# Gathered expert rows: a row is added one panel after its product, and its buffer is filled again one panel after that

## The chip, the cores and the metric

The kernel runs on 1 core of one Trainium2 chip. The metric is the device time of one execution in microseconds (us), the median over runs; lower is better. The engines are called PE (TensorE, matrix products), DVE (VectorE), ACT (ScalarE), POOL (GpSimd) and SP (SyncE, which only issues DMAs here).

## The reference

Two transformer-like blocks run on 512 tokens of width 1024, batch 1, all in float32. The change touches one part of the first block, the product-key experts (PEER). Each token makes 8 queries; each query picks 16 of 16384 experts and has a softmax gate for each pick. An expert is one row of `expert_u` and one row of `expert_v`:

```
u = expert_u[idx]                                   # idx: 128 tokens x 8 heads x 16 picks
v = expert_v[idx]
act = gelu(einsum("thkd,td->thk", u, xt))
out = einsum("thk,thkd->td", gate * act, v)
```

So for each token and each of its 128 picks: the dot product of a row of `expert_u` with the token, a gelu, a product with the gate, and a row of `expert_v` scaled by that number and summed. What comes before (a hybrid of a linear recurrence and convolutions) and after (feed-forward layers, an mLSTM, dilated attention, attention to a memory) is not touched.

## The kernel before

**Two ways to the same sum.** For 384 of the 512 tokens the kernel computes all 16384 experts as dense matrix products and multiplies with a gate table that is zero where nothing was picked. For the other 128 tokens (one on each partition) it gathers the picked rows from memory: 128 picks per token, `PICKS = 128`. The gathered work runs beside the dense work, on engines that the dense work leaves some time.

**The dense work** goes in weight panels of 128 partitions x 1024 floats (512 KB). SP loads panel p into one of 4 places of `weight_ring` (`load_panel`) as soon as POOL is through with panel p-4. ACT copies the panel in two halves to `weight_high`, rounded to fp32r (L249, L251: the split's high part; it may overwrite a place once PE has used panel p-2). POOL subtracts this from the panel and so makes `weight_low`, again in two halves (L277, one pair a panel). PE multiplies the high part with the high and low parts of the input (L291, L292, 16 matmuls) and the low part with the high part of the input (L298, 8 matmuls). A panel is one step.

The gathered work is spread over the steps of three stages, in one count of steps:
- steps 0 to 15, late panels: products with `expert_u`, whose gelu ACT makes and SP stores away (parked);
- steps 16 to 111, parked panels, 12 groups of 8: products with `expert_v`. In each step DVE makes one chunk of the next group's input, by three gate operations (L1592 multiplies a parked activation with its gate, L1596 rounds it to fp32r, L1598 takes the rest; not in the last group), then does its gathered work (`use_rows`), then adds a finished bank to the residual (L1681), for which it waits until PE is through with that panel;
- from step 112, 4 groups of 16: 8 panels of `expert_u`, after each of which ACT makes a gelu and DVE the gates (L1856, L1860, L1862), and 8 of `expert_v`, after each of which DVE adds to the residual (L1873). PE needs all eight gates of a group at its middle.

**The gathered work** of pick k has four parts. Three tables of step numbers, made at L1480 to L1494, say when each stands in its engine's instructions:
- the fetch (`fetch_rows`, L1529), an indirect DMA that POOL issues: for each of 128 tokens a row of 2048 floats (u and v), 1 MB, into buffer k % 4 of `picked_rows`. It stands at step `FETCH_AT[k]`, behind POOL's pair of splits of that step. It waits until the buffer's last user, pick k-4, is added;
- the dot (`use_rows`, L1540), DVE, at step `DOT_AT[k]`;
- gelu and gate (`weigh_rows`, L1555, L1558), ACT, at step `DOT_AT[k] + 1`, behind ACT's split for the next panel. ACT waits for the dot;
- the add (`use_rows`, L1546), DVE, at step `ADD_AT[k]`: the row of v, scaled, is added to a sum in PSUM. It waits for ACT's weight. In a step that has both, the add of the earlier pick stands ahead of the dot.

The step numbers of the dots are spread evenly, with a weight of 0.8 on the parked steps, so that there about three steps in four have a dot.

All engines run through their own instructions in order. They are tied by semaphores only; nothing sets the order but these tables and loops.

Of the kernel before, what the change touches and what calls it, by code (L numbers as in the profile page):

```python
# [1089 lines left out]
PICKS = HEADS * TOPK // COPIES  # L1090
# [5 lines left out]
ROWS = 4  # L1096
# [380 lines left out]
LAST_GROUP_STEP = FIRST_EXPERT_STEP + (EXPERT_GROUPS_LEFT - 1) * 2 * EXPERT_GROUP  # L1477

FIRST_DOT = 5
LAST_DOT = LAST_GROUP_STEP - 2  # L1480
PARKED_SHARE = 0.8


def dot_steps():

    weights = [PARKED_SHARE if LATE_STEPS <= step < FIRST_EXPERT_STEP else 1.0 for step in range(FIRST_DOT, LAST_DOT + 1)]
    reached = np.cumsum(weights) / sum(weights) * (PICKS - 1)
    return [FIRST_DOT + int(np.searchsorted(reached, k + 1e-9)) for k in range(PICKS - 1)] + [LAST_DOT]


DOT_AT = dot_steps()
ADD_AT = [at + 2 for at in DOT_AT]
FETCH_AT = [0] * ROWS + [min(ADD_AT[k - ROWS] + 2, DOT_AT[k]) for k in range(ROWS, PICKS)]
assert all(FETCH_AT[k] <= DOT_AT[k] for k in range(PICKS)) and ADD_AT[-1] == LAST_GROUP_STEP  # L1494


# [26 lines left out]
def fetch_rows(m, pool, io, picked, step):  # L1523

    for k in range(PICKS):
        if FETCH_AT[k] == step:
            if k >= ROWS:
# [6 lines left out]
def use_rows(m, dve, picked, step):  # L1534

    for k in range(PICKS):
        halves = picked.rows[:, k % ROWS, :].rearrange("p (w a n) -> p w a n", w=2, a=2)
        if DOT_AT[k] == step:
# [3 lines left out]
                .then_inc(picked.dotted, 1)  # L1542
        if ADD_AT[k] == step:
            dve.wait_ge(picked.weighed, k + 1)
# [1854 lines left out]
```

## Time and profile before

| | |
|---|---|
| median of 3 runs | 3851.97 us (3847.91 to 3859.61) |
| profiled execution, own time | 3855.03 us |
| its span | 3853.2 us |
| PE busy | 3639.1 us (94%) |
| DVE busy | 2125.1 us (55%) |
| ACT busy | 1509.6 us (39%) |
| POOL busy | 1920.2 us (50%) |
| first and last fetch L1529, start | 856.9 and 1575.3 us |
| first and last add L1546, start | 891.9 and 1591.5 us |

The shares are means over the whole span, in which stages with different limits follow one another; the gathered work lies in less than a fifth of it. Times in the trace are counted from the span's start. The late panels start at about 854 us, the parked panels at 928 us, the last four groups at about 1362 us. Ends of matmuls are modelled, and a POOL operation's span is rough.

### The profile page before, as it was taken

The page shows a single profiled execution, that of the slowest core. Times are in us where ns is not written, and L with a number is a line of the kernel's source. Part 1 is how long each engine was busy: PE and PEld are TensorE (multiplying, and loading weights), DVE is VectorE, ACT ScalarE, POOL GpSimd, SP SyncE. Part 2 cuts the span into 40 slices and gives each one's busy share as a digit, 9 for nine tenths or more (in the row PEclk, how much of TensorE's full clock was granted, in tenths as well). Part 3 has the DMA queues.
Part 4 walks back from the last instruction along what each step waited for, and adds up shares of the span by engine and source line. Part 5 has one row for each costly group of instructions (what it writes and reads, how often), then busy time and mean ns, then how long its engine had stood idle before and what let it go on. Part 6 is the DMA issues. An engine that isn't in the chain of part 4 may idle for free. (4 is left out here: it accounts for less than half of the span.)

```text
span 3853.2 us, 50718 instructions
## 1 busy us (share of the span) xinstructions
PE 3639.1 (94%) x17274; PEld 3077.5 (80%) x17274; DVE 2125.1 (55%) x3418; ACT 1509.6 (39%) x2627; POOL 1920.2 (50%) x1466
## 2 busy tenths in 40 slices
PE   7979999988999999999998998999999999899999
PEld 6457998988999999978886765788878887567887
DVE  7782997866999857663323636433243322554330
ACT  3432555753333333444322434443244422443432
POOL 4623675436787777645541422454445544024444
PEclk9989999999999999999997988999999999799999
DMA  3012453568999989623333211223323233012322
GB/s 130 17 65 82 145 170 128 221 240 330 372 402 404 372 324 339 234 92 98 94 97 111 86 51 39 87 93 94 91 83 96 94 93 120 12 39 87 97 90 92
DMA packets 174247, 569.31 MB, mean 148 GB/s; under 512 B 15377, under 2 KB 59537, under 8 KB 156596
## 3 DMA queue, kind: packets, MB, share of 16 engines
q1 hardware_dynamic: 155700, 433.71, 33.3%
q0 software_dynamic: 18432, 134.23, 8.7%
q8 instruction: 53, 0.87, 0.1%
q14 instruction: 62, 0.51, 0.0%
HBM read 518.33 MB, written 49.55 MB: 147 GB/s over the span
## 5 line engine op out<-in xcount | busy, mean ns | idle before, releaser
L277 POOL TENSOR_TENSOR weight_low<-weight_ring,weight_high 128x512 fp32r<-128x512 f32 x1264 | 1727.2, 1389 | 1781.3 <-ACT weight_high L249 1372.4
L291 PE MATMUL banks<-normed_high,weight_high 128*128 128x512 f32 (+1 forms) x2528 | 949.2, 375 | 38.4 <-ACT weight_high L249 23.4
L292 PE MATMUL banks<-normed_low,weight_high 128*128 128x512 f32 (+1 forms) x2528 | 939.5, 372 | 0.0
L249 ACT ACTIVATE weight_high<-weight_ring 128x512 fp32r<-128x512 f32 x632 | 398.8, 631 | 1363.0 <-PE banks L298 1314.6
L298 PE MATMUL banks<-normed_high,weight_low 128*128 128x512 f32 (+1 forms) x2528 | 572.9, 367 | 6.5 <-POOL weight_low L277 6.2
L291 PEld LDWEIGHTS banks<-normed_high,weight_high 128*128 128x128 f32 x2528 | 483.4, 191 | 108.9 <-issue 35.5
L292 PEld LDWEIGHTS banks<-normed_low,weight_high 128*128 128x128 f32 x2528 | 483.1, 191 | 61.3 <-issue 2.1
L298 PEld LDWEIGHTS banks<-normed_high,weight_low 128*128 128x128 f32 x2528 | 461.4, 188 | 68.9 <-POOL weight_low L277 10.0
L251 ACT ACTIVATE weight_high<-weight_ring 128x512 fp32r<-128x512 f32 (+1 forms) x632 | 389.9, 617 | 93.0 <-PE banks L298 83.0
L2037 DVE TENSOR_TENSOR square<-square,banks 128x512 f32<-128x512 f32 x88 | 60.5, 688 | 416.5 <-PE banks L298 414.9
L291 PE MATMUL banks<-parked_high,weight_high 128*128 128x384 f32 x768 | 261.6, 341 | 17.8 <-ACT weight_high L249 12.3
L292 PE MATMUL banks<-parked_low,weight_high 128*128 128x384 f32 x768 | 260.7, 339 | 0.0
L2059 DVE SCALAR_TENSOR_TENSOR residual<-banks,residual 128x512 f32<-128x512 f32 x32 | 22.1, 692 | 380.2 <-PE banks L298 380.2
L291 PE MATMUL banks<-hidden_high,weight_high 128*128 128x512 f32 x576 | 229.2, 398 | 0.0
L292 PE MATMUL banks<-hidden_low,weight_high 128*128 128x512 f32 x576 | 225.7, 392 | 0.0
L1540 DVE SCALAR_TENSOR_TENSOR picked_rows<-picked_rows,banks 128x1024 f32<-128x1024 f32 x128 | 155.5, 1216 | 47.8 <-DMA picked_rows<-in_expert_rows,picked_experts 47.5
L291 PE MATMUL banks<-middle_high,weight_high 128*128 128x512 f32 x448 | 181.2, 404 | 0.0
L292 PE MATMUL banks<-middle_low,weight_high 128*128 128x512 f32 x448 | 179.5, 401 | 0.0
L1546 DVE SCALAR_TENSOR_TENSOR banks<-picked_rows,picked_weight,banks 128x1024 f32<-128x1024 f32 x128 | 164.1, 1282 | 7.6 <-ACT picked_weight L1558 7.6
L291 PEld LDWEIGHTS banks<-parked_high,weight_high 128*128 128x128 f32 x768 | 145.4, 189 | 19.7 <-ACT weight_high L249 10.4
L1529 POOL DMA_INDIRECT picked_rows<-in_expert_rows,picked_experts x128 | 135.0, 1054 | 42.0 <-DVE banks L1546 23.6
L298 PE MATMUL banks<-parked_high,weight_low 128*128 128x384 f32 x768 | 151.9, 340 | 0.0
(372 smaller groups left out, 5659.9 us busy)
## 6 DMA issues: line engine op xcount, KB each, us to landing
weight_ring<-in_experts SPq DMA_DIRECT2D x256, 512.0 KB, 5.8
weight_ring<-in_ffn_gate SPq DMA_DIRECT2D x88, 512.0 KB, 3.5
weight_ring<-in_ffn_up SPq DMA_DIRECT2D x88, 512.0 KB, 3.5
weight_ring<-in_ffn_down SPq DMA_DIRECT2D x64, 512.0 KB, 3.5
expert_gates<-spread_space SPq DMA_DIRECT2D x6, 4096.0 KB, 12.2
parked_space<-expert_gates SPq DMA_DIRECT2D x24, 768.0 KB, 9.0
parked_space<-parked_activations SPq DMA_DIRECT2D x24, 768.0 KB, 10.9
weight_ring<-in_a_w_in SPq DMA_DIRECT2D x28, 512.0 KB, 3.5
```

What stands on the lines that cost most here:

```text
L249: m.nc.scalar.activation(m.w_hi[:, s % PARTS, 0:HALF], m.ring[:, s, 0:HALF], ACT.Copy).then_inc(m.half_high, 1)
L251: m.nc.scalar.activation(m.w_hi[:, s % PARTS, HALF:width], m.ring[:, s, HALF:width], ACT.Copy).then_inc(m.high, 1)
L277: m.nc.gpsimd.tensor_tensor(m.w_lo[:, s % PARTS, at], m.ring[:, s, at], m.w_hi[:, s % PARTS, at].bitcast(FP), ALU.subtract).then_inc(done, 1)
L291: m.nc.tensor.matmul(out, w_hi, hi(c), start=(first and c == 0), stop=False)
L292: m.nc.tensor.matmul(out, w_hi, lo(c), start=False, stop=False)
L298: ins = m.nc.tensor.matmul(out, w_lo, hi(c), start=False, stop=(last and c == chunks - 1))
L1529: m.nc.gpsimd.indirect_dma_start(picked.rows[:, k % ROWS, :], None, io["expert_rows"], bass.IndirectOffsetOnAxis(ap=picked.expert[:, k:k + ...
L1540: m.nc.vector.scalar_tensor_tensor(out=halves[:, 0], in0=halves[:, 0], scalar=1.0, in1=picked.token, op0=ALU.mult, op1=ALU.mult, accum_out ...
L1546: m.nc.vector.scalar_tensor_tensor(out=picked.total, in0=halves[:, 1], scalar=picked.weight[:, k:k + 1], in1=picked.total, op0=ALU.mult, o ...
L2037: nc.vector.tensor_tensor(tile, tile, m.bank[2 * v + 1][:, :], ALU.mult).then_inc(product.sem, 1)
L2059: ins = nc.vector.scalar_tensor_tensor(out=x, in0=m.bank[c % 4][:, :], scalar=0.5, in1=x, op0=ALU.mult, op1=ALU.add)
```

## The change

The add moves from two steps after its dot to one. The fetch into a buffer moves from two steps after the add that frees it to one step after (or the step of its own dot, where that is earlier). The last dot moves one step later (159 instead of 158), so that the last add stays at step 160; the dots between are spread over one step more.

```diff
--- before.py
+++ after.py
@@ -1477,7 +1477,7 @@
 LAST_GROUP_STEP = FIRST_EXPERT_STEP + (EXPERT_GROUPS_LEFT - 1) * 2 * EXPERT_GROUP
 
 FIRST_DOT = 5
-LAST_DOT = LAST_GROUP_STEP - 2
+LAST_DOT = LAST_GROUP_STEP - 1
 PARKED_SHARE = 0.8
 
 
@@ -1489,8 +1489,8 @@
 
 
 DOT_AT = dot_steps()
-ADD_AT = [at + 2 for at in DOT_AT]
-FETCH_AT = [0] * ROWS + [min(ADD_AT[k - ROWS] + 2, DOT_AT[k]) for k in range(ROWS, PICKS)]
+ADD_AT = [at + 1 for at in DOT_AT]
+FETCH_AT = [0] * ROWS + [min(ADD_AT[k - ROWS] + 1, DOT_AT[k]) for k in range(ROWS, PICKS)]
 assert all(FETCH_AT[k] <= DOT_AT[k] for k in range(PICKS)) and ADD_AT[-1] == LAST_GROUP_STEP
```

In numbers of steps: for pick k the fetch of the buffer's next user stood at dot + 4 and stands at dot + 2. In the parked steps that leaves 3 or 4 steps between a fetch and the dot that uses it, where there were 1 or 2; in the last stage 2 or 3, where there were 0 or 1.

Every engine issues as many instructions of each kind as before. On DVE the rows show steps 17 and 18 (two of the parked steps) before the change. L1592, L1596 and L1598 are the gate operations, L1546 the add, L1540 the dot, L1681 the residual add:

```order
L1592 TENSOR_TENSOR parked_space4<-parked_space4 128x384
L1596 CAST parked_high1<-parked_space4 128x384
L1598 TENSOR_TENSOR parked_low1<-parked_space4,parked_high1 128x384
L1546 SCALAR_TENSOR_TENSOR banks<-picked_rows,picked_weight,banks 128x1024
L1681 TENSOR_TENSOR residual<-residual,banks 128x384
L1592 TENSOR_TENSOR parked_space4<-parked_space4 128x384
L1596 CAST parked_high1<-parked_space4 128x384
L1598 TENSOR_TENSOR parked_low1<-parked_space4,parked_high1 128x384
L1546 SCALAR_TENSOR_TENSOR banks<-picked_rows,picked_weight,banks 128x1024
L1540 SCALAR_TENSOR_TENSOR picked_rows,picked_hidden<-picked_rows,banks 128x1024
L1681 TENSOR_TENSOR residual<-residual,banks 128x384
```

and the same two steps of the changed kernel:

```order
L1592 TENSOR_TENSOR parked_space4<-parked_space4 128x384
L1596 CAST parked_high1<-parked_space4 128x384
L1598 TENSOR_TENSOR parked_low1<-parked_space4,parked_high1 128x384
L1546 SCALAR_TENSOR_TENSOR banks<-picked_rows,picked_weight,banks 128x1024
L1681 TENSOR_TENSOR residual<-residual,banks 128x384
L1592 TENSOR_TENSOR parked_space4<-parked_space4 128x384
L1596 CAST parked_high1<-parked_space4 128x384
L1598 TENSOR_TENSOR parked_low1<-parked_space4,parked_high1 128x384
L1540 SCALAR_TENSOR_TENSOR picked_rows,picked_hidden<-picked_rows,banks 128x1024
L1681 TENSOR_TENSOR residual<-residual,banks 128x384
```

Step 17 has no dot in either table. Before, the step without an add came two steps after the step without a dot; now it comes one step after it, so that a step with an add alone is followed by one with a dot alone.

On POOL the rows show step 0 and what follows up to step 9 and its fetch, before the change (L277 is a half of a panel's split, L1529 a fetch):

```order
L277 TENSOR_TENSOR weight_low<-weight_ring,weight_high 128x512 x2
L1529 DMA picked_rows<-in_expert_rows,picked_experts 128x2048 x4
L277 TENSOR_TENSOR weight_low<-weight_ring,weight_high 128x512 x18
L1529 DMA picked_rows<-in_expert_rows,picked_experts 128x2048
L277 TENSOR_TENSOR weight_low<-weight_ring,weight_high 128x512 x2
```

and of the changed kernel:

```order
L277 TENSOR_TENSOR weight_low<-weight_ring,weight_high 128x512 x2
L1529 DMA picked_rows<-in_expert_rows,picked_experts 128x2048 x4
L277 TENSOR_TENSOR weight_low<-weight_ring,weight_high 128x512 x14
L1529 DMA picked_rows<-in_expert_rows,picked_experts 128x2048
L277 TENSOR_TENSOR weight_low<-weight_ring,weight_high 128x512 x2
```

The first fetch that has to wait for an add stood behind the splits of step 9 and stands behind those of step 7. From there on each fetch stands behind the splits of the step that follows its add's step, and ahead of the splits of the step after that.

## Rows read from the trace of the kernel before

**Rows 1.** windows of the trace, all engines: busy time (instructions), granted clock, DMA share
```profile
1000.00:1050.00 50.00, 50.00 (x286) 50.00 (x286) 49.17 (x73) 19.16 (x40) 40.39 (x34) 1.00 1.01 399
...
928.00:1356.00 428.00, 410.16 (x2304) 408.49 (x2304) 394.98 (x582) 156.86 (x342) 327.16 (x265) 0.98 0.98 382
```

**Rows 2.** timeline of POOL, steady stretch: start us, duration us, then the instruction
```profile
1103.06 2.56 POOL L277 TENSOR_TENSOR weight_low<-weight_ring,weight_high 128x512 fp32r<-128x512 f32 x2 [0.39 <-ACT weight_high L249]
...
1109.98 1.14 POOL L1529 DMA_INDIRECT picked_rows<-in_expert_rows,picked_experts  x1
...
1119.96 1.30 POOL L277 TENSOR_TENSOR weight_low<-weight_ring,weight_high 128x512 fp32r<-128x512 f32 x1 [0.42 <-ACT weight_high L249]
```

**Rows 3.** timeline of DVE, same stretch
```profile
1104.35 1.69 DVE L1592 TENSOR_TENSOR parked_space<-parked_space 128x384 f32<-128x384 f32 x1
...
1106.94 1.28 DVE L1546 SCALAR_TENSOR_TENSOR banks<-picked_rows,picked_weight,banks 128x1024 f32<-128x1024 f32 x1
1108.13 1.22 DVE L1540 SCALAR_TENSOR_TENSOR picked_rows<-picked_rows,banks 128x1024 f32<-128x1024 f32 x1
...
1109.27 0.55 DVE L1681 TENSOR_TENSOR residual<-residual,banks 128x384 f32<-128x384 f32 x1
1109.74 0.55 DVE L1592 TENSOR_TENSOR parked_space<-parked_space 128x384 f32<-128x384 f32 x1
...
1111.19 1.28 DVE L1546 SCALAR_TENSOR_TENSOR banks<-picked_rows,picked_weight,banks 128x1024 f32<-128x1024 f32 x1
```

**Rows 4.** single lines' instructions: duration ns min/median/max
```profile
L1546 DVE SCALAR_TENSOR_TENSOR banks<-picked_rows,picked_weight,banks x128: 1274/1283/1290, 891.9 to 1591.5; 128x1024 f32<-128x1024 f32 x128
...
L1592 DVE TENSOR_TENSOR parked_space<-parked_space x96: 542/553/1697, 860.5 to 1319.8; 128x384 f32<-128x384 f32 x96
...
L1596 DVE CAST parked_high<-parked_space x96: 359/360/3058, 861.1 to 1321.5; 128x384 fp32r<-128x384 f32 x96
```

**Rows 5.** the page's costliest groups: busy us, mean ns, idle before and its main releaser
```profile
L1540 DVE SCALAR_TENSOR_TENSOR picked_rows<-picked_rows,banks 128x1024 f32<-128x1024 f32 x128 | 155.5, 1216 | 47.8 <-DMA picked_rows<-in_expert_rows,picked_experts 47.5
...
L1529 POOL DMA_INDIRECT picked_rows<-in_expert_rows,picked_experts x128 | 135.0, 1054 | 42.0 <-DVE banks L1546 23.6
```

**Rows 6.** waits, 1362 to 1600 us: waiting line, releasing line, us, times, longest
```profile
PE banks L291 <- DVE expert_low L1862: 6.6, 3, 3.5
...
PE banks L291 <- ACT weight_high L249: 4.6, 3, 2.8
```

**Rows 7.** timeline of DVE after the hand-over to the parked panels
```profile
948.28 1.28 DVE L1546 SCALAR_TENSOR_TENSOR banks<-picked_rows,picked_weight,banks 128x1024 f32<-128x1024 f32 x1
...
953.51 1.28 DVE L1546 SCALAR_TENSOR_TENSOR banks<-picked_rows,picked_weight,banks 128x1024 f32<-128x1024 f32 x1
...
955.74 3.06 DVE L1596 CAST parked_high<-parked_space 128x384 fp32r<-128x384 f32 x1
...
959.31 1.28 DVE L1546 SCALAR_TENSOR_TENSOR banks<-picked_rows,picked_weight,banks 128x1024 f32<-128x1024 f32 x1
...
993.77 1.17 DVE L1592 TENSOR_TENSOR parked_space<-parked_space 128x384 f32<-128x384 f32 x1
...
996.83 1.28 DVE L1546 SCALAR_TENSOR_TENSOR banks<-picked_rows,picked_weight,banks 128x1024 f32<-128x1024 f32 x1
...
1005.37 1.28 DVE L1546 SCALAR_TENSOR_TENSOR banks<-picked_rows,picked_weight,banks 128x1024 f32<-128x1024 f32 x1
```

**Rows 8.** timeline of POOL, same stretch
```profile
955.05 0.96 POOL L1529 DMA_INDIRECT picked_rows<-in_expert_rows,picked_experts  x1 [0.34 <-DVE banks L1546]
956.03 2.54 POOL L277 TENSOR_TENSOR weight_low<-weight_ring,weight_high 128x512 fp32r<-128x512 f32 x2
...
993.24 2.86 POOL L277 TENSOR_TENSOR weight_low<-weight_ring,weight_high 128x512 fp32r<-128x512 f32 x2 [1.19 <-ACT weight_high L249]
```

**Rows 9.** timeline of DVE, a group of the last stage, first and last add
```profile
1445.53 1.28 DVE L1546 SCALAR_TENSOR_TENSOR banks<-picked_rows,picked_weight,banks 128x1024 f32<-128x1024 f32 x1
...
1476.34 1.28 DVE L1546 SCALAR_TENSOR_TENSOR banks<-picked_rows,picked_weight,banks 128x1024 f32<-128x1024 f32 x1
```

## The prediction

> **What bounds the kernel now.** I read the windows of the profile first. The change touches only the steps in which rows are gathered, from about 857 to 1592 us of the span. In the middle of that stretch TensorE (PE) has no gap: 286 matmuls in 50 us, with VectorE (DVE) busy 49.17 of 50 us and the DMA engines at a share of 1.01 [rows 1]. A panel is 24 matmuls, so 24 x 50 / 286 = 4.20 us; POOL, which splits one panel for each that PE works on, starts a pair of splits at 1103.06 and, four panels later, at 1119.96 [rows 2]: 4.22 us a panel, which I use. The stretch of the 96 parked panels takes 428 us with PE busy 410.16 [rows 1]. PE is the bound there, but DVE stands right behind it.
>
> Second, the DVE timeline of a step in which it adds one pick and dots another, start to start: the add 1.19 us (1106.94 to 1108.13), the dot 1.14, the residual add L1681 0.47, then the three gate operations of the next step 1.45, which end where the next add starts: 4.25 us in all, already 0.03 over the panel [rows 3]. It is made good in the steps without an add or without a dot.
>
> Third, what shares a resource with DVE. The gate operations L1592 and L1596 usually take 553 and 360 ns, but at worst 1697 and 3058 ns; the add, which has one operand in PSUM, lies between 1274 and 1290 ns in all 128 cases [rows 4]. The long ones lie on GpSimd (POOL) splits: L1592 started at 1104.35 takes 1.69 us and ends 0.42 us after the pair of splits that ran from 1103.06 for 2.56 us [rows 2, 3]. So a gate operation and a split exclude each other. In the steady stretch they mostly miss each other: the gate operations at 1109.74 lie under the fetch that POOL issues from 1109.98 [rows 2, 3], and the next split comes when DVE is at its add again. This phase is what the change moves.
>
> **The change part by part.** The number of dots, adds, fetches, splits and matmuls is the same; every price is one of position.
>
> (a) The fetch of a buffer moves from 4 steps behind its last dot to 2, and from 0 to 2 steps ahead of the dot that uses it to 2 to 4. DVE waited 47.5 us for rows [rows 5]. Nearly all of it goes. On PE it shows only where it makes ScalarE (ACT), which waits for the dot, late with a panel, or the gates late: 4.6 and 6.6 us in the last four groups, of which late rows are a part [rows 6]. Worth 0 to 11 us by itself. I take 0, since in the sum below PE waits for something later than the rows.
>
> (b) The add comes one step after its dot. It waits for the weight that ACT makes in that same step, behind its own split for the next panel. DVE has by then gone through L1681 and three gate operations, longer than ACT's two copies and two small activations. I take 0; in the steps without gates, where the add may have to wait, DVE has 1.4 us a step to spare (add, dot and L1681 are 2.80 of 4.22 us [rows 3]).
>
> (c) The fetch at POOL's step s+1 now waits for the add of DVE's step s, no longer for that of s-1. Behind the fetch on POOL stand the two splits of panel s+2; behind them the next load of that ring place. This is the dear part. From rows in which POOL did wait for the add: add at 953.51, fetch at 955.05, splits from 956.03 [rows 7, 8]. So with the add's start as zero, the fetch starts at 1.54 and the splits run from 2.52 for at least 2.54 us, to 5.06. DVE starts the next gates at 1.19 + 1.14 + 0.47 = 2.80 in a step with add and dot, and at 1.19 + 0.47 = 1.66 in a step with an add alone. The splits of s+2 are not held by ACT or PE (both are ahead), so in every gathered step with gates the splits fall on the gates. They can't slide apart: the fetch follows the add, and the splits follow the fetch.
>
> What a collision costs, from rows:
> - add alone: 953.51 to 959.31, 5.80 us; the cast L1596 at 955.74 was held for 3.06 us, through both splits [rows 7, 8].
> - add and dot: L1592 starts 0.28 us into the splits. At 993.77 it started 0.53 us into a pair begun at 993.24, and the next add came at 996.83, 3.59 us after the splits' start [rows 7, 8]. So 2.52 + 3.59 = 6.11; with the longer fetches seen (mean 1054 ns against the 0.96 us of this one [rows 5, 8]) I take 6.15.
> - dot alone: own work 1.14 + 0.47 + 1.45 = 3.06. POOL has no fetch in between and does the splits of two panels in a row, so part of them hold a gate operation; between 0 and the 1.14 us by which the L1592 at 1104.35 was stretched I take 0.85: 3.9 us.
>
> Steps 16 to 103 have gates. By the new table 44 have both, 22 an add alone, 22 a dot alone: a cycle of four is 2 x 6.15 + 5.80 + 3.9 = 22.0 us against 4 x 4.22 = 16.88. Excess 5.1 x 22 = 112 us. Part of that is paid already: after DVE's wait for the first parked gates, the adds of steps 16 to 28 take from 948.28 to 1005.37, 57.1 us for 12 steps instead of 50.6 [rows 7]. 112 - 6.5 = 106 us.
>
> In the last four groups the first eight steps have gates. Their seven intervals took 30.8 us in one of them (1445.53 to 1476.34 [rows 9]); by the prices above, one add alone, one dot alone and five of both are 5.80 + 3.9 + 30.75 = 40.5. PE needs the eighth gate at the group's middle, so it waits the difference, 9.7 us, in three groups (the fourth has no picks left): 29 us. The other eight steps have no gates: 0. The first 16 steps have none either: POOL's splits come up to 2.52 us behind an add there too, but they are for a panel that PE starts only after the one it works on: 0. If that cover were gone, it would be at most 2.5 us in each of 9 steps, 23 in all.
>
> **Sum:** 106 + 29 = 135 us. The profiled execution took 3855.0 us, so 3990; the median of the runs shown is 3852.0, 3 us lower: **3987 us**, 3.5% slower.
>
> The Trainium skill (SBUF — State Buffer, "SBUF: two separate sides") says of VectorE and GpSimd that their shared ports are "an exclusive lock, not a bandwidth split", held for one instruction, the loser blocked. This rule speaks against the change, and the trace agrees as far as L1592 goes. By it alone the cast would be let in after the first of two splits; the row has it held over both (3.06 us). By the rule a cycle is 22.0 us or a little less; by the row, where four splits follow one another, the cast could stay out 1.7 us longer, 23.7.
>
> **Bounds of the collision.** Least: DVE takes the port after the first split and keeps it for all three operations: add and dot 2.52 + 1.28 + 1.45 = 5.25, add alone 3.80 + 0.90 (1.45 less L1592's 0.55) = 4.70, dot alone 3.06: cycle 18.3, 1.4 x 22 - 6.5 = 24 us, and 34.1 - 30.8 = 3.3 in each of three last groups: 3886. Most: 23.7 a cycle, 6.8 x 22 - 6.5 = 143, and 9.7 + 2 x 1.7 = 13 in each of the three: 4034.
>
> **The rivals.**
> - *The collision is there, but short-lived* (0.11). For it: before the change DVE and POOL also met so after 948 us, and it ended by itself within 12 steps. Against: then the fetch depended on an add a step further back. If it ends so at each group of eight, 6.5 us for some cases only: 3 to 6 times 6.5, 3872 to 3891, slower.
> - *Hidden* (0.05). The splits start after the gates, since POOL waits for ACT instead. Then the wait for rows is gone and PE still sets the pace: within 0.3%, 3842 to 3863.
> - *Faster* (0.06). The same, and the saved waits reach PE. Place: the last four groups, and the hand-over at 928 to 985 us. Price: the 11 us of [rows 6], and some 5 us at the hand-over if the parked gates land sooner: 3836. It decides if in a step with add and dot the splits start later than 4.25 us behind the add, when the gates are over; the rows say 2.52.
> - *The lock-step holds* (0.78), my forecast: 3886 to 4034.
>
> **Numbers.** Predicted time 3987. Runs of this kernel differ by some 0.3%, so less than that (12 us) can't be told from no change. Faster 0.06, same 0.05, slower 0.89. The range takes the forecast's cases and most of the first rival: 3870 to 4040.
>
> **What would show it.** In the profile after: the fetch L1529 waits for the add L1546 some 100 times, together over 200 us instead of 23.6; L1592 and L1596 have a much longer mean; DVE's waits for rows fall below 10 us; adds in the parked steps stand 6.1 us apart; PE idles over 1 us a panel, before L298 for the splits, and the parked stretch lasts some 530 us instead of 428. Wrong would be the forecast if the splits there start only after the gates, or if DVE gets its three operations in between the two splits of a pair. The granted clock, 1.00 in the steady stretch [rows 1], may fall there too; a panel of 4.22 us has 1.3 us of room in a step of 5.5 for that.

## The result, and the profile after

The changed kernel takes 4042.37 us (median of 4 runs, 4041.45 to 4049.12) against 3851.11 us for the kernel before beside it: a ratio of 1.050, 95% interval 1.048 to 1.052. It is 5.0% slower. The forecast was 3987 us, 3.5% slower, with 4040 as its upper end: the sign came out and so did the place of the loss, but it is 191 us where 135 were forecast.

The page of the profile after, its first rows and four groups:

```profile
span 4039.8 us, 50718 instructions
...
PE 3706.2 (92%) x17274; PEld 3105.9 (77%) x17274; DVE 2328.3 (58%) x3418; ACT 1501.1 (37%) x2627; POOL 1897.7 (47%) x1466
...
L291 PE MATMUL banks<-parked_high,weight_high 128*128 128x384 f32 x768 | 272.3, 355 | 50.7 <-DVE parked_low L1598 43.8
...
L1529 POOL DMA_INDIRECT picked_rows<-in_expert_rows,picked_experts x128 | 123.2, 962 | 358.7 <-DVE banks L1546 356.7
...
L298 PE MATMUL banks<-parked_high,weight_low 128*128 128x384 f32 x768 | 180.6, 373 | 64.2 <-POOL weight_low L277 63.9
...
L1555 ACT ACTIVATE picked_active<-picked_hidden 128x1 f32<-128x1 f32 x128 | 25.9, 202 | 461.1 <-DVE picked_rows L1540 457.1
```

The fetch L1529 waits 356.7 us for the add, where it waited 23.6 [rows 5]. PE now waits where it did not before: 63.9 us for the split's low half, 43.8 us for the gates. DVE shows 203 us more busy time with as many instructions: it was not given more work, its instructions last longer. The durations (min/median/max ns) of single lines of the kernel after say which ones:

```profile
L1592 DVE TENSOR_TENSOR parked_space<-parked_space x96: 548/555/2715, 862.3 to 1469.9; 128x384 f32<-128x384 f32 x96
L1596 DVE CAST parked_high<-parked_space x96: 359/360/5566, 862.9 to 1472.5; 128x384 fp32r<-128x384 f32 x96
L1598 DVE TENSOR_TENSOR parked_low<-parked_space,parked_high x96: 557/559/5823, 863.2 to 1472.9; 128x384 fp32r<-128x384 f32 x96
L1546 DVE SCALAR_TENSOR_TENSOR banks<-picked_rows,picked_weight,banks x128: 1277/1283/1291, 893.9 to 1781.6; 128x1024 f32<-128x1024 f32 x128
```

The cast that took 3.06 us at worst [rows 4] takes up to 5.57, while the add, with an operand in PSUM, is never held. (The 5.82 us of L1598 are not new: the kernel before has such a row too, shown below, in the section on the prediction.) One cycle of four steps on DVE (start us, duration us; the numbers in brackets, in POOL's rows below, are the idle time before the row and its releaser):

```profile
1105.68 1.28 DVE L1546 SCALAR_TENSOR_TENSOR banks<-picked_rows,picked_weight,banks 128x1024 f32<-128x1024 f32 x1
...
1112.07 1.28 DVE L1546 SCALAR_TENSOR_TENSOR banks<-picked_rows,picked_weight,banks 128x1024 f32<-128x1024 f32 x1
1113.26 1.21 DVE L1540 SCALAR_TENSOR_TENSOR picked_rows<-picked_rows,banks 128x1024 f32<-128x1024 f32 x1
...
1114.86 2.71 DVE L1592 TENSOR_TENSOR parked_space<-parked_space 128x384 f32<-128x384 f32 x1
...
1118.48 1.28 DVE L1546 SCALAR_TENSOR_TENSOR banks<-picked_rows,picked_weight,banks 128x1024 f32<-128x1024 f32 x1
...
1120.72 5.51 DVE L1596 CAST parked_high<-parked_space 128x384 fp32r<-128x384 f32 x1
...
1126.74 1.21 DVE L1540 SCALAR_TENSOR_TENSOR picked_rows<-picked_rows,banks 128x1024 f32<-128x1024 f32 x1
...
1129.80 1.28 DVE L1546 SCALAR_TENSOR_TENSOR banks<-picked_rows,picked_weight,banks 128x1024 f32<-128x1024 f32 x1
```

and POOL beside it:

```profile
1113.62 0.96 POOL L1529 DMA_INDIRECT picked_rows<-in_expert_rows,picked_experts  x1 [2.88 <-DVE banks L1546]
1114.60 2.55 POOL L277 TENSOR_TENSOR weight_low<-weight_ring,weight_high 128x512 fp32r<-128x512 f32 x2
1120.04 0.96 POOL L1529 DMA_INDIRECT picked_rows<-in_expert_rows,picked_experts  x1 [2.88 <-DVE banks L1546]
1121.02 4.99 POOL L277 TENSOR_TENSOR weight_low<-weight_ring,weight_high 128x512 fp32r<-128x512 f32 x4
1131.36 0.96 POOL L1529 DMA_INDIRECT picked_rows<-in_expert_rows,picked_experts  x1 [5.35 <-DVE banks L1546]
```

Read them together. The add starts at 1112.07; 1.55 us later the fetch, 2.53 later the splits, as the forecast had it. L1592, begun 0.26 us into the splits, ends 0.42 us after both of them. The two steps with add and dot take 6.39 and 6.41 us. At 1118.48 comes the add alone; behind its fetch POOL does *four* halves in a row, and the cast stays out for all four: 8.26 us. The step with a dot alone meets no split: 3.06 us. The cycle is 24.12 us, where PE's own pace is 16.88.

Windows of the kernel after (columns as in [rows 1]), the steady stretch, and the parked stretch up to its last panel:

```profile
1100.00:1150.00 50.00, 41.64 (x205) 39.19 (x204) 49.45 (x51) 11.88 (x28) 27.64 (x24) 0.90 0.81 287
929.00:1508.00 579.00, 463.84 (x2311) 429.45 (x2309) 543.47 (x581) 143.55 (x339) 311.02 (x265) 0.93 0.79 283
```

DVE is the bound now, busy 49.45 of 50 us, with 51 instructions in them instead of 73. PE's loss has two parts: it idles 579 - 463.8 = 115 us instead of 18 [rows 1], and its 2311 matmuls take 0.201 us each instead of 0.178, 52 us in all, at a granted clock of 0.93 instead of 0.98. In this stretch the clock is a consequence: DVE, which PE waits for, has next to no gap, and none of the DVE or POOL times above hangs on PE.

In what follows "parked" is the time from the first matmul of the parked panels (L291) to the last one (L298), and "last stage" from there to the last matmul of the last groups' `expert_v` panels. Before: 427.3 and 297.7 us. After: 577.5 and 336.0, so +150.2 and +38.3.

### The profile page after: what moved, and what is told of

It reads as the page before. It is cut to its first block and busy times, and to the rows that moved or that the text cites. A ratio compares the mean times of both kernels' runs of the same rounds, so it can differ in the third digit from the quotient of the medians.

```text
span 4039.8 us, 50718 instructions
## 1 busy us (share of the span) xinstructions
PE 3706.2 (92%) x17274; PEld 3105.9 (77%) x17274; DVE 2328.3 (58%) x3418; ACT 1501.1 (37%) x2627; POOL 1897.7 (47%) x1466
## 5 line engine op out<-in xcount | busy, mean ns | idle before, releaser
L277 POOL TENSOR_TENSOR weight_low<-weight_ring,weight_high 128x512 fp32r<-128x512 f32 x1264 | 1717.0, 1382 | 1674.3 <-ACT weight_high L249 1263.4
L291 PE MATMUL banks<-normed_high,weight_high 128*128 128x512 f32 (+1 forms) x2528 | 951.2, 376 | 34.4 <-ACT weight_high L249 18.9
L298 PE MATMUL banks<-normed_high,weight_low 128*128 128x512 f32 (+1 forms) x2528 | 580.5, 370 | 28.0 <-POOL weight_low L277 27.7
L291 PEld LDWEIGHTS banks<-normed_high,weight_high 128*128 128x128 f32 x2528 | 485.4, 192 | 104.6 <-issue 34.8
L298 PEld LDWEIGHTS banks<-normed_high,weight_low 128*128 128x128 f32 x2528 | 461.9, 189 | 98.6 <-POOL weight_low L277 39.8
L291 PE MATMUL banks<-parked_high,weight_high 128*128 128x384 f32 x768 | 272.3, 355 | 50.7 <-DVE parked_low L1598 43.8
L1529 POOL DMA_INDIRECT picked_rows<-in_expert_rows,picked_experts x128 | 123.2, 962 | 358.7 <-DVE banks L1546 356.7
L298 PE MATMUL banks<-parked_high,weight_low 128*128 128x384 f32 x768 | 180.6, 373 | 64.2 <-POOL weight_low L277 63.9
L291 PE MATMUL banks<-hidden_high,weight_high 128*128 128x512 f32 x576 | 229.2, 398 | 0.0
L298 PEld LDWEIGHTS banks<-parked_high,weight_low 128*128 128x128 f32 x768 | 145.3, 206 | 88.6 <-POOL weight_low L277 88.5
L291 PEld LDWEIGHTS banks<-parked_high,weight_high 128*128 128x128 f32 x768 | 152.3, 198 | 60.4 <-DVE parked_low L1598 48.0
L1555 ACT ACTIVATE picked_active<-picked_hidden 128x1 f32<-128x1 f32 x128 | 25.9, 202 | 461.1 <-DVE picked_rows L1540 457.1
L291 PE MATMUL banks<-middle_high,weight_high 128*128 128x512 f32 x448 | 181.8, 406 | 0.0
## 6 DMA issues: line engine op xcount, KB each, us to landing
expert_gates<-spread_space SPq DMA_DIRECT2D x6, 4096.0 KB, 12.2
```

Of the source, the lines that this page charges most:

```text
L277: m.nc.gpsimd.tensor_tensor(m.w_lo[:, s % PARTS, at], m.ring[:, s, at], m.w_hi[:, s % PARTS, at].bitcast(FP), ALU.subtract).then_inc(done, 1)
L291: m.nc.tensor.matmul(out, w_hi, hi(c), start=(first and c == 0), stop=False)
L298: ins = m.nc.tensor.matmul(out, w_lo, hi(c), start=False, stop=(last and c == chunks - 1))
L1529: m.nc.gpsimd.indirect_dma_start(picked.rows[:, k % ROWS, :], None, io["expert_rows"], bass.IndirectOffsetOnAxis(ap=picked.expert[:, k:k + ...
L1555: m.nc.scalar.activation(picked.active[:, k:k + 1], picked.hidden[:, k:k + 1], ACT.Gelu_apprx_tanh)\
```

## The experiments

Two theories. A, of the prediction: the fetch waits for an add only one step back, so POOL's splits start 2.5 us behind the add and lie on the gates. B, the rival: the weight is late, since the add comes one step after the dot, and DVE waits for it. C came up on the way: an operation of DVE that has begun before the splits keeps them off. Further rivals (D to G) are named in the expectations where they are tested; that of experiment 3 calls another one C.

**1. The add moved alone.** The add one step after the dot, as in the change, the fetch two steps after the add, as before:

```diff
-FETCH_AT = [0] * ROWS + [min(ADD_AT[k - ROWS] + 1, DOT_AT[k]) for k in range(ROWS, PICKS)]
+FETCH_AT = [0] * ROWS + [min(ADD_AT[k - ROWS] + 2, DOT_AT[k]) for k in range(ROWS, PICKS)]
```

> The add stays one step behind its dot, but the fetch goes back to two steps behind the add. Theory A (the fetch directly behind the add puts POOL's splits on DVE's gate operations, and the port they share makes each wait for the other): POOL no longer waits for the add of the step before, the collisions go, and the time is near that of before, 3840 to 3860 us. Rival B (the add now waits for a weight that ACT makes in the same step, and ACT in turn for the dot): that is unchanged here, so the time stays near 4042 us.

Measured: 3851.23 us, ratio 1.001 [0.9995, 1.0025]. The loss is gone, with B's part still in place; DVE's adds wait 21.9 us for weights over all 128 picks, and the kernel takes as long as before. DVE has no wait for rows left (47.5 us before [rows 5]), and the last stage is 13.7 us *shorter* than before: PE idles 7.1 us less in it, and its matmuls take 6.5 us less, at a granted clock of 1.00 instead of 0.97. It is given back in the parked stretch, 12.2 us longer: PE's waits grow by 6.6 us, its matmuls take 5.0 us more at a clock of 0.97 instead of 0.98. There the first parked inputs land later (DVE waits 15.9 us for them instead of 11.7), and the collisions that follow the hand-over last longer: a cycle of four steps, 16.9 us where nothing collides, takes 20.3 us five times and 18.8 once, from 950 to 1071 us; before the change the long ones were 20.3, 19.3 and 17.5, from 948 to 1005 us. So the collision of the hand-over ends by itself here too, but later.

**2. The fetch moved alone.** The kernel before, with the fetch one step after the add:

```diff
-FETCH_AT = [0] * ROWS + [min(ADD_AT[k - ROWS] + 2, DOT_AT[k]) for k in range(ROWS, PICKS)]
+FETCH_AT = [0] * ROWS + [min(ADD_AT[k - ROWS] + 1, DOT_AT[k]) for k in range(ROWS, PICKS)]
```

> The table of before (add two steps behind its dot, last dot at step 158), and only the fetch moved to one step behind the add. Theory A: the full loss comes back, since a cycle of four steps has one add alone (5.8 us), one dot alone (3.1), one add and dot at 6.4 and one add and dot whose gate operations lie on four splits in a row (9.0): 24.3 us, 4020 to 4050 us. Rival B: the add waits for nothing, as before, so 3845 to 3860 us.

Measured: 4037.63 us, 1.049 [1.046, 1.052]: the whole loss, with parked at 577.0 us and the last stage at 336.9. From POOL's and then DVE's timeline of this kernel:

```profile
1105.88 5.05 POOL L277 TENSOR_TENSOR weight_low<-weight_ring,weight_high 128x512 fp32r<-128x512 f32 x4
```

```profile
1106.13 5.21 DVE L1592 TENSOR_TENSOR parked_space<-parked_space 128x384 f32<-128x384 f32 x1
```

With the add two steps behind the dot the four halves fall on a step with add and dot, so L1592 is held and not the cast. The price is the same: a run of four halves is sat out. With experiment 1, B is out.

**3. The wait moved, the instructions not.** The changed kernel with five row buffers and the fetches where they stand. Each now waits for the add of pick k-5, one pick further back. Room for the fifth buffer comes from scratch tensors that lie idle then (in lines not shown, gelu and weight are also written over the dot's result, and one copy on DVE falls away):

```diff
-ROWS = 4
+ROWS = 5
...
-FETCH_AT = [0] * ROWS + [min(ADD_AT[k - ROWS] + 1, DOT_AT[k]) for k in range(ROWS, PICKS)]
+FETCH_AT = [0] * 4 + [min(ADD_AT[k - 4] + 1, DOT_AT[k]) for k in range(4, PICKS)]
...
-        buffers = space.take(SLOTS, DENSE)
+        buffers = Places([m.sum[:, 0:DENSE], m.square[:, 0, 0:DENSE], m.square[:, 1, 0:DENSE], space.take(DENSE)])
```

> All operations at the steps of the changed kernel, but five row buffers instead of four (room made by putting three parking buffers into idle tensors), so that each fetch waits for the add of the pick before the one that it waited for, at least one step further back. Theory A: POOL's wait for the add and with it the collisions go, 3835 to 3860 us. Rival B: unchanged, near 4042 us. Rival C (fetches that start earlier crowd the DMA queues, so that panels land late): unchanged too, near 4042 us.

Measured: 3836.74 us, 0.997 [0.995, 0.999]. The fetch's place costs nothing; what costs is that it waits for an add just made. B is out once more, and so is C of the expectation, crowded DMA queues. Parked 430.8 us, last stage 279.1 (18.6 shorter than before).

**4. Gates right behind the add.** In the changed kernel DVE's order in a parked step is now add, gates, dot, so that the gates are over (2.6 us behind the add) about when the splits start:

```diff
                     for c in range(E):
+                        use_rows(m, dve, picked, U + g * E + c, dots=False)
                         if g < PARKED - 1:
...
                             gate(dve, g + 1, (g + 1) % 2, c)
-                        use_rows(m, dve, picked, U + g * E + c)
+                        use_rows(m, dve, picked, U + g * E + c, adds=False)
```

> The changed kernel's tables, but in the parked steps DVE does its gate operations between the add and the dot instead of behind the dot and the residual add. POOL still waits for the add directly. Theory A: the gate operations end 2.64 us behind the add's start, when the splits have begun 0.12 us before, so in the parked steps nearly no collision is left; the 150 us lost there go, the 38 us lost in the last four groups stay: 3880 to 3900 us. Rival D (not the collision, but POOL's wait for the add itself makes PE late): the wait is as long, so over 4000 us.

Measured: 4062.63 us, 1.056 [1.053, 1.059], worse than the change itself. The expectation failed, and shows why in two rows of this kernel, POOL's and DVE's:

```profile
1155.70 2.53 POOL L277 TENSOR_TENSOR weight_low<-weight_ring,weight_high 128x512 fp32r<-128x512 f32 x2
```

```profile
1155.27 3.38 DVE L1598 TENSOR_TENSOR parked_low<-parked_space,parked_high 128x384 fp32r<-128x384 f32 x1
```

L1598, 0.56 us by itself, began 0.43 us ahead of the splits, had not ended by 0.13 us, and ended 0.42 us after both. So C is wrong as far as the recorded starts go: having begun first doesn't help DVE. POOL's spans are rough, though, and the trace doesn't show when the port changes hands, so that POOL may have had it before its recorded start. This run leaves D open, the theory that POOL's wait for the add is itself what makes PE late.

**5. The same, and the splits wait for the gates.** Experiment 4 with one wait on POOL, ahead of each pair, for the gates that DVE makes at that time:

```diff
                 for k in range(U + N):
+                    if 0 <= k - 2 - U < N - E:
+                        pool.wait_ge(gated, 2 * E + k - 2 - U + 1)
                     split_low_panel(m, pool, u_first + k, k % SLOTS)
```

> As e4_gates_after_add, and POOL starts the splits of panel s+2 only when DVE has finished the gate operations of step s, some 0.3 us later than before. In e4 the last gate operation, L1598, started 0.43 us ahead of the splits, was not finished when they began, and was held over both (3.4 us). Theory A, put more sharply (a gate operation that is still running when a pair of splits begins is held until POOL pauses): now none is caught, DVE needs about 4.3 us for a step with add and dot, the parked steps run at PE's pace; only the 38 us of the last four groups are left: 3880 to 3900 us. Rival D (the fetch's and so the splits' wait for the add makes PE late, whatever DVE meets): the wait is even longer, 4000 us or more.

Measured: 3890.52 us, 1.011 [1.009, 1.012]. Timeline of POOL, then of DVE:

```profile
1135.67 1.02 POOL L1529 DMA_INDIRECT picked_rows<-in_expert_rows,picked_experts  x1 [0.67 <-DVE banks L1546]
1136.92 2.55 POOL L277 TENSOR_TENSOR weight_low<-weight_ring,weight_high 128x512 fp32r<-128x512 f32 x2 [0.23 <-DVE parked_low L1598]
```

```profile
1134.11 1.29 DVE L1546 SCALAR_TENSOR_TENSOR banks<-picked_rows,picked_weight,banks 128x1024 f32<-128x1024 f32 x1
...
1136.28 0.56 DVE L1598 TENSOR_TENSOR parked_low<-parked_space,parked_high 128x384 fp32r<-128x384 f32 x1
...
1138.58 1.29 DVE L1546 SCALAR_TENSOR_TENSOR banks<-picked_rows,picked_weight,banks 128x1024 f32<-128x1024 f32 x1
```

POOL waits 0.23 us, and a hold of 2.8 us is gone. Against experiment 4 that is 172 us, though every pair starts later than there and POOL still waits 142.2 us for adds: D is out, it is what DVE meets that costs. Parked is 428.1 us, as before the change. The last stage, which the edit doesn't touch, keeps its loss (332.1).

**6. The change in the last groups only.** The fetch one step behind adds from step 112 on, two behind the others:

```diff
-FETCH_AT = [0] * ROWS + [min(ADD_AT[k - ROWS] + 1, DOT_AT[k]) for k in range(ROWS, PICKS)]
+FETCH_AT = [0] * ROWS + [min(ADD_AT[k - ROWS] + (1 if ADD_AT[k - ROWS] >= FIRST_EXPERT_STEP else 2), DOT_AT[k]) for k in range(ROWS, PICKS)]
```

> The changed kernel, but only the fetches whose awaited add lies at step 112 or later stand one step behind it; all others stand two behind. Theory A by stages: the last four groups' loss alone, 38 us: 3883 to 3893 us. Rival E (the time lost in the last groups comes from a backlog that the parked steps hand over): near 3852 us.

Measured: 3898.96 us, 1.012 [1.010, 1.014], 6 us above what was expected. The last stage alone is 31.6 us longer than before, near the 29 of the forecast, so the loss there is not a backlog of the parked steps (E of the expectation); the parked stretch is 15 us longer, of the kind seen in experiment 1 (DVE waits 17.4 us for its first parked inputs), which the expectation had left out. Experiment 1 differs from this one by the last groups' fetches alone, and beside it the last stage is 45.4 us longer: the place of these fetches costs more than the 31.6 us, since it also swallows the 13.7 that experiment 1 gains there.

**7. A pause between the halves.** The changed kernel; POOL waits between the two halves of a pair until DVE has made the gates of that time. If DVE gets in at any pause of POOL's, a step is one half shorter:

```diff
         pool.wait_ge(ready, p + 1)
+        if between and done is m.low:
+            between()
         m.nc.gpsimd.tensor_tensor(m.w_lo[:, s % PARTS, at], ...
...
-                    split_low_panel(m, pool, u_first + k, k % SLOTS)
+                    gates = 2 * E + k - U if 0 <= k - 1 - U < N - E else None
+                    split_low_panel(m, pool, u_first + k, k % SLOTS, between=gates and (lambda: pool.wait_ge(gated, gates)))
```

> The changed kernel (operations of DVE in its order), and POOL waits between the two splits of panel k until DVE has finished the gate operations of step k-1. The number of collisions stays: each pair still begins on a gate operation. Theory A, with the hold ending where POOL pauses: a step with add and dot takes 2.52 + 1.28 + 1.45 = 5.25 us instead of 6.4, an add alone and a dot alone 8.75 together instead of 11.3; a cycle of four 19.3 us against 16.9, so 22 x 2.4 - 6.5 = 46 us in the parked steps and 38 in the last groups: 3925 to 3945 us. Rival F (the hold is over the time that POOL has splits at hand, pause or not): 4030 us or more. Rival D (POOL's waits make PE late): more than 4042 us.

Measured: 3935.07 us, 1.022 [1.020, 1.024]. On POOL, then on DVE (the lines are two further down in this kernel: L1594 is the product with the gate, L1548 the add):

```profile
1133.94 1.31 POOL L279 TENSOR_TENSOR weight_low<-weight_ring,weight_high 128x512 fp32r<-128x512 f32 x1
1136.81 1.30 POOL L279 TENSOR_TENSOR weight_low<-weight_ring,weight_high 128x512 fp32r<-128x512 f32 x1 [1.56 <-DVE parked_low L1600]
```

```profile
1131.30 1.28 DVE L1548 SCALAR_TENSOR_TENSOR banks<-picked_rows,picked_weight,banks 128x1024 f32<-128x1024 f32 x1
...
1134.09 1.58 DVE L1594 TENSOR_TENSOR parked_space<-parked_space 128x384 f32<-128x384 f32 x1
...
1136.58 1.28 DVE L1548 SCALAR_TENSOR_TENSOR banks<-picked_rows,picked_weight,banks 128x1024 f32<-128x1024 f32 x1
```

Steps with add and dot are 5.28 us, where the prediction's lower bound for "let in after the first half" said 5.25, and the parked stretch is 44 us longer than before, where 46 were expected. Where there is a pause, DVE takes it. So the hold does not last over all the work that POOL has left (F of the expectation).

**8. Parked inputs fetched earlier.** Experiment 3, with SP's fetch of the second group's parked inputs and gates moved up into the late panels:

```diff
                 for k in range(U):
+                    if k == 8:
+                        fetch(1, 0)
                     load_panel(m, sp, u_first + SLOTS + k, k % SLOTS, panel(io["experts"], U0 + SLOTS + k))
...
-                fetch(1, 0)
```

> e3_five_buffers, and SP fetches the first parked inputs of the second group at step 8 instead of behind the last store of step 15. In e3 DVE waited 15.3 us for them, ACT stood behind DVE's dot, and PE idled 11.3 and 3.2 us. If that hand-over wait is what is left, 15 to 22 us go: 3815 to 3825 us. If PE is held there by something else (the DMA queues are full at a share near 1), no change: 3837 us.

Measured: 3830.56 us, 0.994 [0.991, 0.996]. DVE's wait of 15.3 us at the hand-over is gone, and PE's waits in 929 to 1353 us, which were 11.3 for ACT and 6.4 for the gates, now read:

```profile
PE banks L291 <- DVE parked_low L1606: 8.7, 3, 4.2
PE banks L291 <- ACT weight_high L249: 1.5, 2, 0.8
```

The parked stretch is 9.4 us shorter than in experiment 3, the median 6.2 us, less than half of the 15 to 22 that were expected. This is the fastest version found, together with the last one.

**9. A pause only ahead of a lone pair.** The changed kernel; POOL waits for the gates only where a pair has no fetch ahead of it, that is in the middle of each run of four halves:

```diff
                 for k in range(U + N):
+                    if 0 <= k - 2 - U < N - E and k - 1 not in FETCH_AT:
+                        pool.wait_ge(gated, 2 * E + k - 2 - U + 1)
                     split_low_panel(m, pool, u_first + k, k % SLOTS)
```

> The changed kernel, and before a pair of splits that has no fetch ahead of it POOL waits until DVE has finished the gate operations of two steps back. So four splits never stand in a row any more; all other collisions stay. This is the term that was priced too low. Theory A: an add alone takes 5.8 us again instead of 8.26; the pair then starts 0.2 us behind the gate operations and holds the next L1592 by about 1.1, so a dot alone takes 4.2 instead of 3.06; a cycle of four is 22.8 instead of 24.1 us, 22 x 1.3 = 29 us less than the changed kernel: 4005 to 4020 us. Rival G (the excess over the forecast has another source, the granted clock or the port after a fetch): 4035 us or more.

Measured: 4006.93 us, 1.041 [1.039, 1.044]: 35 us of the loss hang on the runs of four. DVE's timeline, from an add alone to the dot of the step after, and the adds behind:

```profile
1152.15 1.28 DVE L1546 SCALAR_TENSOR_TENSOR banks<-picked_rows,picked_weight,banks 128x1024 f32<-128x1024 f32 x1
...
1154.39 3.02 DVE L1596 CAST parked_high<-parked_space 128x384 fp32r<-128x384 f32 x1
...
1157.92 1.21 DVE L1540 SCALAR_TENSOR_TENSOR picked_rows<-picked_rows,banks 128x1024 f32<-128x1024 f32 x1
...
1161.96 1.28 DVE L1546 SCALAR_TENSOR_TENSOR banks<-picked_rows,picked_weight,banks 128x1024 f32<-128x1024 f32 x1
...
1168.32 1.28 DVE L1546 SCALAR_TENSOR_TENSOR banks<-picked_rows,picked_weight,banks 128x1024 f32<-128x1024 f32 x1
```

Here the steps are near what the prediction had priced: add alone 5.77 (predicted 5.80), dot alone 4.04 (3.9), and with add and dot 6.36 (6.15); a cycle of 22.5 us. The parked stretch, 543.6 us, is 116 us longer than before, where the forecast had 106. G of the expectation, another source for the excess such as the clock, is out for these 35 us.

**10. All together.** Experiment 8 with the order and the wait of experiment 5.

> e8_early_parked_inputs with DVE's gate operations between add and dot and POOL's splits behind them, as in e5_gates_then_splits. PE still idles 8.7 us for gates and 6.9 us for ACT in e8. If collisions in the parked steps cause a part of that, 5 to 10 us go: 3820 to 3827 us. If not, 3830 us, or some us more, since POOL now waits for DVE in each step and the add for ACT's weight.

Measured: 3830.30 us, 0.995 [0.993, 0.997]: nothing on top of experiment 8 that the medians can tell. In the two profiled executions PE idles 5.5 us in the parked stretch instead of 10.3, and the stretch is 413.5 us instead of 421.4; one execution each doesn't show that this is worth anything.

## Why the prediction was right in kind and short in size

- **(c), the fetch waits for the add one step back, and the splits fall on the gates:** right, and shown. Experiment 2 has it alone with all of the loss; experiment 3 takes the wait away at unchanged places, and the loss is gone. The offsets (fetch 1.54, splits 2.52 us behind the add) measured 1.55 and 2.53.
- **The price of the collisions, "22.0 us" a cycle of four:** this is the step that failed. Measured 24.12: add alone 8.26 (not 5.80), dot alone 3.06 (not 3.9), add and dot 6.40 (not 6.15). The prediction had seen that POOL does the splits of two panels in a row, and that "where four splits follow one another, the cast could stay out 1.7 us longer", but it charged that run to the dot-alone step, at 0.85 us, as if only the end of it would touch an operation. That the cast stays out for all four stands there only in the upper bound, 23.7 a cycle. Experiment 9 cuts the run of four in the middle, and the cycle comes down to 22.5, with add alone and dot alone near their predicted prices. Over 22 cycles the run of four is some 35 us of what was missing.
- **A row that the prediction did not use** has the price in the kernel before. Of the three gate operations it read the longest times of L1592 and L1596, not that of L1598. DVE, then POOL:

```profile
861.51 5.82 DVE L1598 TENSOR_TENSOR parked_low<-parked_space,parked_high 128x384 fp32r<-128x384 f32 x1
```

```profile
861.92 8.11 POOL L277 TENSOR_TENSOR weight_low<-weight_ring,weight_high 128x512 fp32r<-128x512 f32 x6
```

L1598 began 0.41 us ahead of a run of six halves and ended at 867.33, 0.43 us after the fourth of them (its end is 866.90). It shows both things that were learned later: a hold over four halves, and an operation held that had begun first.

- **The step with add and dot, 6.15:** too low by 0.25, 11 us over 22 cycles, since the row behind it was of another kind. In the pair at 993.24 [rows 8] DVE was let in between the halves: L1592, 1.17 us [rows 7], ended 0.42 us after the first half, the second half took 1.61 us instead of 1.29 (hence 2.86 for the pair), and the cast was held over that one. So the next add came 3.59 us after the pair's start; here, with L1592 held for 2.7 us over both, it is 3.88.
- **When DVE is let in:** the trace has no pause of POOL between the halves at 993.24, so a hold that lasts until POOL pauses is not the whole of it. What differs is ACT: it finished the copy that the second half reads at 993.80, 0.56 us *after* the first half had begun; for the pair of the changed kernel at 1114.60 it had been finished 4.90 us before. (In the run of six above, the fifth half's input was finished at 866.78, after the fourth had begun, and there DVE was let in.) In the kernels before and after together a gate operation waited across 135 such boundaries between two halves. Where the next half's input lay ready when the half ahead of it began, it stayed out in 117 of 119; where it became ready later, it was let in in 16 of 16. Why that decides is not shown. The wait for the add, once it ends, finds both halves ready, and so this change turns POOL's pairs into the kind that is not let go.
- **Parked, +106:** with the measured cycle of 24.12 the same sum gives 7.24 x 22 - 6.5 = 153; the stage grew by 150.2.
- **Last groups, +29:** 38.3 measured, 31.6 in experiment 6, which has this part alone. The seven intervals of one group run from the add at 1610.85 to the one at 1653.28, 42.4 us where 40.5 were forecast (five of 6.37, and 10.6 for the add alone and the dot alone together, not 9.7). Less the 30.8 of before that is 11.6 a group. By halves of a group, the three with `expert_u` panels took 138.2 us instead of 109.3, which is the 29 of the forecast, though PE spends its wait there on POOL's splits (22.2 us, 0 before) and not only on the gates at the middle (12.2 instead of 7.3). The three with `expert_v` panels, which the forecast put at 0, took 121.2 instead of 111.9: PE waited 4.7 us longer for the last gates, and its matmuls took 4.5 us longer, at granted clocks of 0.92, 0.96 and 0.89 instead of 1.00, 0.95 and 0.96. There, apart from that wait, PE is never idle, so that the lower clock counts.
- **(a), waits for rows:** gone to the last one, as forecast; "0 to 11" was too narrow for what they are worth (13.7 to 18.6 us of the last stage in experiments 1 and 3). It counted PE's waits alone, which fell by 7.1 and 12.4 us; the matmuls got 6.5 and 6.1 us shorter beside that, at a granted clock of 1.00 and 0.99 instead of 0.97. Taking 0 in this sum was right, since PE waits for DVE anyway.
- **(b), the add's wait for the weight, 0:** right. 23.6 us over 15 adds, in a kernel where it delays nothing; experiment 1 shows it harmless.
- **The first 16 steps, 0:** right. The parked panels start at 930.0 instead of 928.8 us.
- **How long the lock is held:** by the Trainium skill (SBUF — State Buffer, "SBUF: two separate sides") whichever engine starts first gets the shared ports for its whole instruction, so DVE would be let in between two halves, and an operation that began first would be through. The traces disagree with both where the halves lie ready: L1598 began first by the recorded starts and was held (experiment 4), and DVE is held over two halves (2.7 us) or four (5.5). They agree with the first where the second half was not ready yet (993.24). The measurement decides.
- **"PE idles before L298 for the splits":** the wait is there (63.9 us), and beside it one for the gates (43.8) that the text had not named. PE waits for whichever of the two is late; both hang on the same DVE step. Adds 6.1 us apart: 6.4. Parked stretch "some 530 us": 577.5. The clock did fall, to 0.90, and cost nothing of its own in the parked steps, as the 1.3 us of room had it; in the last groups it cost the 4.5 us above.

The upper bound, 4034, came from a cycle of 23.7 us, with the run of four priced as it turned out; the real one lies 0.4 us above, 9 us over 22 cycles, by the two steps with add and dot.

## What to carry to other kernels

When an engine's instruction is made to wait for a recent one of another engine, everything that stands behind it on its queue gets a fixed phase to that event: work out what the other engine does at that time, and whether the two share something. Price a hold by how many operations stand back to back and ready on the engine that holds, not by one of them, and take the price from a row of the same kind: look for the longest time of *every* instruction that can be held. In the parked steps a pause of 0.2 us in the right place (experiment 5, with the gates moved up) took the hold away, and an extra buffer that makes the wait an old one (experiment 3) did so in the last groups too. A fetch's position and the age of what it waits for are two choices: the kernel with the earlier fetches was some 13 us faster than before (experiment 3), once they no longer tied POOL to an add just made.

## What the runs showed of the hardware

- A gate operation of DVE (operands in SBUF) that meets POOL's splits, both halves ready, is held over all of them: L1592 takes 2.7 us over two halves of 1.28 and 5.2 over four, the cast 3.06 and 5.5. L1592 and L1598 end some 0.4 us after the last half, the cast 0.2.
- It is let in after a half when the next one's input became ready only after that half had begun (16 of 16 in the kernels before and after), and stays out when it was ready (117 of 119), though the trace shows no pause of POOL in either case. The half behind then mostly takes some 1.6 us instead of 1.28.
- It is held even when its recorded start is 0.43 us ahead of the splits' (3.38 us instead of 0.56, experiment 4), while a wait of 0.23 us of POOL's, so that its start falls behind the operation's end, frees it (experiment 5).
- The add and L1540, with an operand in PSUM, are held in none of 128 cases each: in the kernel before they take 1274 to 1290 and 1205 to 1223 ns, though 117 and 108 of them lie beside splits.
- POOL's fetch (0.95 to 1.34 us of its time in the kernel before) holds no gate operation: there the gate operations from 1109.74 on lay under the fetch from 1109.98 and had their usual length [rows 2, 3].
